# The third pair's weights loaded as six whole chunks in place of 22 halves and pieces

## The chip, the cores and the metric

One NeuronCore of a Trainium2 chip runs the kernel. The metric is the time on the device in microseconds; lower is better.

## What is computed

One inference step of a decoder layer, for a prompt of 256 positions and 8 sample rows, width 1024, all in float32. First come a combined input projection, a short gated convolution, a windowed attention and an output projection. Then comes a mixture of experts: each row chooses 4 of 32 experts, and each expert is an up-projection of 1024 x 2048, a clamped SwiGLU and a down-projection of 1024 x 1024:

```
u = xb @ w_up[e] + b_up[e]
glu = jnp.minimum(u[:, 0::2], SWIGLU_LIMIT)
lin = jnp.clip(u[:, 1::2], -SWIGLU_LIMIT, SWIGLU_LIMIT)
a = glu * jax.nn.sigmoid(SWIGLU_ALPHA * glu) * (lin + 1)
return a @ w_down[e] + b_down[e]
```

The results of an expert are weighted by its gate and added to the rows that chose it. The change is in the loading of the experts' weights, 32 x 12 MiB = 403 MB.

## The kernel before

The experts are worked through in 16 pairs, g = 0 to 15. A pair's weights are six chunks of 4 MiB: four of the up-projections (two for each expert) and two of the down-projections. A chunk is 128 partitions x 32 KB, and it is used in two halves, j = 0 to 11 in a pair: half j is chunk j // 2, its first or second 16 KB of every partition. On TensorE `up(j)` reads j = 0 to 7 (L2009) and `down(e, h)` reads j = 8 to 11 (L2076). Both ask `loaded(j)` (L1975) to wait for the half; between them stand the gathering of the next pair's rows, the transposes and the scattering of results, in an order written out by hand (L2182 to L2238).

**Four places.** In SBUF there are places for four chunks (`unit(u)`, L347): three in the tile `ring`, one in `area`. Chunk number `turn`, counted from the second pair on, takes the place `UNIT[turn % 4]`, so it can be loaded when the chunk four ahead of it has been read. All loads are issued by SP on one queue, in the order of use, and each waits on SP for a semaphore that counts releases by TensorE, `ring_free`. A release is signalled by the matmul that comes after the last read of a half or, from the third pair on, of a chunk (`frees(j)`, L1996).

**How the loads are cut.** SP has a section for each kind of pair:

- The first pair (g = 0, L605 to L638) is loaded in halves, two of them in smaller parts.
- The second pair (g = 1, L639 to L649) is loaded in halves (16 KB of each partition), but its j = 10 and 11 in two pieces each.
- The third pair (g = 2, L650 to L664) is loaded in pieces and halves. Its chunks 0 to 3 take the places that the second pair's chunks 2 to 5 leave. Its chunks 4 and 5 take the places of its own chunks 0 and 1. `EARLY` (L209) tells in how many pieces: 4 for the second half of chunk 0, which follows j = 5, and 2 for each other half. `early` (L585) issues each piece but the last when the matmuls that read that much of the place are through (`early_free`); the last one waits for `ring_free`. The halves of chunks 4 and 5 wait for `chunk_free` and `ring_free`.
- The pairs g = 3 to 14 run in a loop (`pair`, L598): each chunk is one DMA, whole, after one wait.
- The last pair is loaded in halves and in rows (`LAST_ROWS`, L212), so that the last matmuls can follow the last bytes.

The second pair in `pair()` on TensorE has `halves=True, pair1=True` (L2293), the third `halves=True, pair2=True` (L2294); both wait for each half and, where there are pieces, for `early_piece` (L1984).

Of the kernel before, what the change touches and what calls it, by code (L numbers as in the profile page):

```python
# [56 lines left out]
PAIR_CHUNKS = UP_CHUNKS + DOWN_CHUNKS  # L57
# [9 lines left out]
UNIT = [1, 2, 3, 0]  # L67
UNITS_KEPT = len(UNIT)
ODD, EVEN = 0, -PAIR_CHUNKS
assert 2 * PAIR_CHUNKS % UNITS_KEPT == 0  # L70
PAIRS2_TURNS = 2 * PAIR_CHUNKS // UNITS_KEPT
HALF_PAIRS = (1, 2)
PAIR1_FREED = HALF_FREED + len(FIRST_PLACE)
LOOP_FREED = PAIR1_FREED + 2 * PAIR_CHUNKS - PAIR_CHUNKS

# [130 lines left out]
OUTPUTS = [(0, 0), (1, 0), (0, 1), (1, 1)]  # L206


EARLY = {2: 2, 3: 2, 4: 2, 5: 4, 6: 2, 7: 2, 8: 2, 9: 2, 10: 2, 11: 2}  # L209


LAST_ROWS = {7: (2, 2), 8: (2, 2), 9: (2, 2), 10: (2, 2), 11: (2, 1, 1)}  # L212
# [23 lines left out]
def build(nc, x_prompt, x_sample, state_conv, cache_k, cache_v, rel_bias, attn_norm_w, w_in, conv_w, q_norm_w,  # L236
          k_norm_w, sinks, w_out, ffn_norm_w, w_router, b_router, w_up, b_up, w_down, b_down, consts,
          y_prompt, y_sample, conv_prompt, k_prompt, v_prompt, conv_sample, k_sample, v_sample):
    with ExitStack() as ctx:
# [3 lines left out]
        def sem(name):  # L243
            return ctx.enter_context(nc.semaphore(name))
# [165 lines left out]
        ring_free = sem("ring_free")  # L410
        first_loaded = [sem(f"first_loaded{j}") for j in range(2 * PAIR_CHUNKS)]
        unit_half = [sem(f"unit_half{u}") for u in range(UNITS_KEPT)]
# [84 lines left out]
        last_piece = {(j, n): sem(f"last_piece{j}_{n}") for j, rows_ in LAST_ROWS.items() for n in range(len(rows_) - 1)}  # L497
        y_first = sem("y_first")
        early_free = sem("early_free")
        chunk_free = sem("chunk_free")  # L500
        first_free = sem("first_free")
        early_piece = {j: sem(f"early_piece{j}") for j in EARLY}
        sample_cleared = sem("sample_cleared")
# [36 lines left out]
        def _(sp):  # L540
# [12 lines left out]
            for c in range(2, FIRST_CHUNKS):  # L553
# [4 lines left out]
                else:  # L558
                    n = c - W_IN_CHUNKS
# [19 lines left out]
            def half(b, i, turn, h):  # L579

                u = UNIT[turn % UNITS_KEPT]
                f = slice(SLOT * h, SLOT * h + SLOT)
                sp.dma_start(unit(u)[:, f], rows_of(b, i)[:, f]).then_inc((unit_half, unit_full)[h][u], 16)

            def early(b, i, turn, h, j, freed):  # L585

                u = UNIT[turn % UNITS_KEPT]
                size = SLOT // EARLY[j]
                for n in range(EARLY[j]):
                    f = slice(SLOT * h + size * n, SLOT * h + size * n + size)  # L590
                    if n == EARLY[j] - 1:
                        sp.wait_ge(ring_free, freed)
                        sp.dma_start(unit(u)[:, f], rows_of(b, i)[:, f]).then_inc((unit_half, unit_full)[h][u], 16)
                    else:
                        sp.wait_ge(early_free, sum(EARLY.get(c, 1) - 1 for c in range(j)) + n + 1)
                        sp.dma_start(unit(u)[:, f], rows_of(b, i)[:, f]).then_inc(early_piece[j], 16)
# [42 lines left out]
            for b in range(PAIR_CHUNKS):  # L639
                for h in range(2):  # L640
                    if b < UNITS_KEPT:
                        sp.wait_ge(ring_free, FREED[2 + 2 * b + h])
                    else:
                        j = 2 * (b - UNITS_KEPT) + h
# [5 lines left out]
            for b in range(PAIR_CHUNKS):  # L650
                turn = PAIR_CHUNKS + b
                freed = turn - UNITS_KEPT
                for h in range(2):
                    j = 2 * freed + h
                    if j in EARLY:
                        early(b, 2, turn, h, j, PAIR1_FREED + j + 1)
                        continue
                    if freed < PAIR_CHUNKS:
                        sp.wait_ge(ring_free, PAIR1_FREED + j + 1)
                    elif h == 0:  # L660
                        sp.wait_ge(chunk_free, freed - PAIR_CHUNKS + 1)
                    else:
                        sp.wait_ge(ring_free, LOOP_FREED + freed + 1)
                    half(b, 2, turn, h)  # L664
            with sp.Fori(1, PAIRS // 2 - 1) as h:
                pair(h, 1, h * 2 + 1)
                pair(h + 1, 0, h * 2 + 2)
            for b in range(PAIR_CHUNKS):
                turn = 2 * PAIR_CHUNKS * (PAIRS // 2 - 1) + ODD + b
                sp.wait_ge(ring_free, LOOP_FREED + turn - UNITS_KEPT + 1)  # L670
                u = UNIT[turn % UNITS_KEPT]
                for h in range(2):
                    j = 2 * b + h
# [905 lines left out]
        def _(pe):  # L1579
# [32 lines left out]
            for what, a in STEPS:  # L1612
                if what == "anorm":
                    tr(misc_bank()[:, 0:KT], rows[V_ANORM:V_ANORM + KT, :]).then_inc(misc_full, 1)
                elif what == "s_cols":
                    b = misc_bank()
                    pe.wait_ge(x_sample_loaded, 16)
                    for k in range(KT):
                        mm = tr(b[:, DEC * k:DEC * k + DEC], x[0:DEC, 2, 128 * k:128 * k + 128])
                    mm.then_inc(misc_full, 1)  # L1620
                    for m, h in TURNS:
                        pe.wait_ge(x_loaded[m][h], 16)
                        for k in range(4 * h, 4 * h + 4):
                            o = 1024 * m + 128 * k
                            mm = tr(pA[:, o:o + 128], x[:, m, 128 * k:128 * k + 128])
                        mm.then_inc(x_halves, 1)
                elif what == "rstd":
                    b = misc_bank()
                    pe.wait_ge(norm_inv, 1)
                    for m, (t0, r) in enumerate(TOK):  # L1630
                        mm = matmul(b[:, t0:t0 + r], stat[0:r, 12 + m:13 + m].to_broadcast([r, 128]), ident[0:r, 0:r])
# [7 lines left out]
                elif what == "tile":  # L1639
                    kind, c, j, t = TILES[a]  # L1640
# [9 lines left out]
                    for k in range(KT):  # L1650
                        if c == 0:
# [5 lines left out]
                            mm = matmul(pB[:, a % 2, 0:NT], w, xw[:, k, :], start=(k == 0), stop=(k == KT - 1))  # L1657
# [7 lines left out]
                        if kind != "q":  # L1665
                            w = ring[:, place(c), :].rearrange("p (k n) -> p k n", k=KT)[:, k, 128 * j:128 * j + 128]
                            mm = matmul(pB[:, a % 2, 0:NT], w, hT[:, k, :], start=(k == 0), stop=(k == KT - 1))
# [4 lines left out]
                        for h in range(2):  # L1672
                            mm = matmul(pB[HD * h:HD * h + HD, a % 2, 0:NT], w[:, k, h, HD * j:HD * j + HD],
                                        hT[:, k, :], start=(k == 0), stop=(k == KT - 1))
# [287 lines left out]

            pe.wait_ge(bias_cast, SPLITS)

            def pair(g, pairs2, odd, kind, halves=False, pair1=False, pair2=False, left_over=None):
                first, last = kind == "first", kind == "last"
                base = {"first": PRE_FILLS, "over": OVER_BASE + PAIR_FILLS * g}.get(kind, PAIR_BASE + PAIR_FILLS * g)
                parity = {"first": PRE_FILLS, "over": OVER_BASE}.get(kind, PAIR_BASE) % 2
# [6 lines left out]
                def loaded(j, whole=False):  # L1975

                    b, h = j // 2, j % 2
                    if first:
                        pe.wait_ge(first_loaded[j], {8: 64, 9: 32}.get(j, 16))
                        return first_place(j)  # L1980
                    turn = (ODD if odd else EVEN) + b
                    u = UNIT[turn % UNITS_KEPT]
                    early_j = PAIR_CHUNKS * 2 * (g - 1) + j - 2 * UNITS_KEPT if halves else -1
                    if early_j in EARLY:  # L1984
                        pe.wait_ge(early_piece[early_j], 16 * (EARLY[early_j] - 1))
                    if last and j in LAST_ROWS and not whole:
                        pe.wait_ge(last_piece[j, 0], 16)
                    elif (last or halves) and h == 0:
                        n = 1 + len(HALF_PAIRS) * PAIR_CHUNKS // UNITS_KEPT if last else 1
                        at_ = turn if last else PAIR_CHUNKS * (g - 1) + b  # L1990
                        pe.wait_ge(unit_half[u], 16 * (n + at_ // UNITS_KEPT))
                    elif last or halves or h == 0:
                        pe.wait_ge(unit_full[u], 16 * PAIRS2_TURNS * pairs2 + 16 * (turn // UNITS_KEPT + 1))
                    return unit(u)[:, SLOT * h:SLOT * h + SLOT]
# [14 lines left out]
                def up(j, freed=False):  # L2009

                    e = j // UP_CHUNKS
                    c = j % UP_CHUNKS
                    if first and e == 0:
                        if c == 1:
                            first_turn(2)
                            first_turn(3)
                        pe.wait_ge(misc_free, FILL["x_turn", c])
                    elif j in (0, 2):
                        pe.wait_ge(misc_free, base - 1 + j // 2 - (1 if pair1 else 0))
                    w = loaded(j)  # L2020
                    for k in (2 * c, 2 * c + 1):
                        if last and j in LAST_ROWS and k % 2:
                            loaded(j, whole=True)
                        row = w[:, 2048 * (k % 2):2048 * (k % 2) + 2048]
                        for n in range(2):
                            for a in range(2):
                                mm = matmul(up_out(e, a, n), xsT[:, k, 64 * e:64 * e + 64], columns_of(row, a, n),
                                            start=(k == 0), stop=(k == KT - 1))
                                if freed and k == 2 * c and n == a == 0:
                                    mm.then_inc(ring_free, 1)  # L2030
                                if first and j == 0 and a and n == 0:
                                    mm.then_inc(first_free, 1)
                                if pair1 and a and EARLY.get(j) == 4 and (k % 2, n) != (1, 1):
                                    mm.then_inc(early_free, 1)
                        if pair1 and EARLY.get(j) == 2 and k % 2 == 0:
                            mm.then_inc(early_free, 1)
                        if first and j == k == 0:
                            mm.then_inc(ring_free, 1)
                        elif first and j == 1 and k == 2:
                            mm.then_inc(first_free, 1)  # L2040
                    if c == UP_CHUNKS - 1:
                        mm.then_inc(up_done, 1)
                    elif frees(j):
                        mm.then_inc(ring_free, 1)
                    elif pair2 and j in (0, 2):
                        mm.then_inc(chunk_free, 1)

                def y_rows(e, a):

# [241 lines left out]

            left_over = pair(0, 0, 0, "first")
            pair(1, 0, 1, "steady", halves=True, pair1=True, left_over=left_over)  # L2293
            pair(2, 1, 0, "steady", halves=True, pair2=True)  # L2294
            with pe.Fori(1, PAIRS // 2 - 1) as h:
                pair(h * 2 + 1, h, 1, "steady")
                pair(h * 2 + 2, h + 1, 0, "steady")
# [44 lines left out]
```

## Time and profile before

| | |
|---|---|
| time, median of 3 runs | 1174.58 us (1174.53 to 1174.8) |
| profiled execution: its span | 1172.1 us (no other time of it is given) |
| TensorE busy | 1121.6 us, 96% |
| VectorE, ScalarE, GpSimd busy | 35%, 16%, 1% |
| DMA | 442.03 MB, mean 377 GB/s |
| mean granted TensorE clock | 0.994 of full speed |

The span goes from the first to the last instruction. The profile's page has busy shares over the whole span and in 40 equal slices; TensorE's share there is modelled, so 96% is not 96% of what the engine can do. The other views are answers of the trace: windows (busy time, DMA share and GB/s in any stretch), the waits of an engine and what ended them, the chain of waits (the work that ended last, followed back), the list of instructions in time, and the DMA issues with the time until their data had landed. A DMA is spread over 16 DMA engines and has landed when the last of them is through.

### The profile page before, as it was taken

What the parts mean: (1) busy time and instruction counts of PE and PEld (TensorE: products, weight loads), DVE (VectorE), ACT (ScalarE), POOL (GpSimd) and SP (SyncE); (2) the same over time, 40 slices, a digit from 0 to 9 for tenths busy, and PEclk for the clock granted to TensorE, in tenths of its full rate; (3) what the DMA queues carried; (4) which work ended last, traced back from release to release, by engine and by line L of the source; (5) the groups of instructions that cost most, each with busy time, mean ns of one, the idle gap of its engine ahead of it and who ended that gap; (6) DMA issues with size and microseconds to landing.
All of it is one profiled execution on the core that took longest, in us unless ns stands there. A gap on an engine that the chain in (4) does not pass through costs nothing.

```text
span 1172.1 us, 14019 instructions
## 1 busy us (share of the span) xinstructions
PE 1121.6 (96%) x5671; PEld 502.1 (43%) x5671; DVE 414.4 (35%) x848; ACT 191.4 (16%) x363; POOL 16.5 (1%) x31
## 2 busy tenths in 40 slices
PE   9999999999999999999999999999999999999998
PEld 6688888663333333333333333333333333333332
DVE  4763354663263323323131323232323232322222
ACT  2123213431042010101011111111010101010101
POOL 1200001000000000000000000000000000000000
PEclk9999999999999999999999999999999999999999
DMA  9945325839999999999999999999999999999997
GB/s 318 372 168 179 130 88 201 342 127 397 428 420 423 431 428 431 430 430 432 431 431 435 433 433 431 431 432 429 435 434 432 431 432 431 431 433 434 426 422 289
DMA packets 41870, 442.03 MB, mean 377 GB/s; under 512 B 3890, under 2 KB 9266, under 8 KB 24828
## 3 DMA queue, kind: packets, MB, share of 16 engines
q1 hardware_dynamic: 39336, 435.08, 88.7%
q0 software_dynamic: 1648, 5.83, 1.6%
q10 hardware_dynamic: 852, 0.64, 0.2%
q8 instruction: 26, 0.43, 0.1%
q14 instruction: 8, 0.07, 0.0%
HBM read 440.23 MB, written 2.36 MB: 378 GB/s over the span
## 4 chain that ended last, share of the span: by engine, by line
PE 60%; DMA 36%; DVE 2%; ACT 1%; issue 0%; SPq 0%; ACTq 0%
PE pA L1589 26%; PE pB L1589 26%; DMA ring<-in_w_up 18%; DMA ring<-in_w_down 12%; PE pM L1589 6%; DMA area<-in_w_up 5%; PE pM L1592 1%; PE pA L1592 1%; DMA rows<-in_attn_norm_w 0%; ACT area L942 0%; DVE hn L1483 0%; DVE x L1441 0%; DVE area L1485 0%; DVE area L1477 0%; DVE area L1020 0%
## 5 line engine op out<-in xcount | busy, mean ns | idle before, releaser
L1589 PE MATMUL pA<-ring,hn 128*64 128x512 f32 x1536 | 352.6, 602 | 23.4 <-DMA ring<-in_w_up 23.4
L1589 PEld LDWEIGHTS pA<-ring,hn 128*64 128x64 f32 x1536 | 105.2, 137 | 219.3 <-issue 185.5
L1589 PE MATMUL pB<-area,ring 128*128 128x264 f32 (+1 forms) x928 | 184.6, 388 | 0.3 <-ACT area L794 0.3
L1589 PE MATMUL pB<-ring,area 128*64 128x512 f32 (+2 forms) x784 | 171.5, 591 | 7.1 <-DMA ring<-in_w_down 5.8
L1589 PEld LDWEIGHTS pB<-area,ring 128*128 128x128 f32 (+1 forms) x928 | 143.6, 175 | 34.4 <-issue 3.0
L1589 PE MATMUL pA<-area,hn 128*64 128x512 f32 x512 | 119.3, 610 | 10.4 <-DMA area<-in_w_up 10.4
L1589 PEld LDWEIGHTS pB<-ring,area 128*64 128x64 f32 (+2 forms) x784 | 58.6, 136 | 101.9 <-issue 89.0
L1441 DVE TENSOR_TENSOR x<-pM,x 128x512 f32<-128x512 f32 x60 | 40.1, 691 | 147.3 <-PE pM L1589 147.2
L930 ACT ACTIVATE area<-area 128x512 f32<-128x512 f32 x30 | 18.9, 630 | 385.2 <-DVE area L1424 385.2
L1356 DVE COPY conv_row<-pM 128x512 f32<-128x512 f32 x30 | 20.6, 686 | 146.4 <-PE pM L1589 146.4
L1589 PE MATMUL pB<-area 128*64 128x512 f32 (+2 forms) x300 | 66.9, 549 | 1.2 <-DVE area L1007 1.2
L1589 PEld LDWEIGHTS pA<-area,hn 128*64 128x64 f32 x512 | 36.1, 139 | 74.6 <-issue 59.7
L1589 PE MATMUL pM<-area 128*128 128x512 bf16 (+2 forms) x368 | 52.4, 330 | 1.5 <-DVE x L1441 1.4
L1424 DVE TENSOR_SCALAR area<-pA 128x512 f32<-128x512 f32 x30 | 20.7, 691 | 92.6 <-PE pA L1589 92.6
L1359 DVE TENSOR_TENSOR hn<-pM,fnorm 128x512 f32<-128x512 f32 x30 | 20.7, 691 | 84.9 <-PE pM L1592 84.4
L1466 DVE COPY area<-pB 64x512 f32<-64x512 f32 x15 | 10.4, 694 | 101.5 <-PE pB L1589 101.5
L1589 PEld LDWEIGHTS pM<-area 128*128 128x128 bf16 (+2 forms) x368 | 18.7, 96 | 52.4 <-issue 35.6
L1589 PE MATMUL pM<-hn,x 128*128 128x512 bf16 (+1 forms) x120 | 37.4, 396 | 0.0
L1589 PEld LDWEIGHTS pB<-area 128*64 128x64 f32 (+2 forms) x300 | 20.8, 131 | 35.3 <-issue 30.7
L1592 PEld LDWEIGHTS pA<-cst,area 128*128 128x128 f32 x168 | 22.2, 190 | 24.8 <-issue 24.3
L942 ACT ACTIVATE area<-pA 128x512 f32<-128x512 f32 x15 | 9.0, 597 | 120.7 <-PE pA L1592 120.7
L1592 PE MATMUL pA<-cst,area 128*128 128x128 f32 x168 | 28.3, 299 | 0.0
(307 smaller groups left out, 788.0 us busy)
## 6 DMA issues: line engine op xcount, KB each, us to landing
ring<-in_w_up SPq DMA_DIRECT2D x36, 4096.0 KB, 29.8
ring<-in_w_down SPq DMA_DIRECT2D x18, 4096.0 KB, 29.1
area<-in_w_up SPq DMA_DIRECT2D x12, 4096.0 KB, 30.2
ring<-in_w_up SPq DMA_DIRECT2D x17, 2048.0 KB, 13.3
area<-in_w_down SPq DMA_DIRECT2D x6, 4096.0 KB, 30.0
ring<-in_w_in SPq DMA_DIRECT2D x22, 1024.0 KB, 12.7
ring<-in_w_up SPq DMA_DIRECT2D x14, 1024.0 KB, 9.3
ring<-in_w_down SPq DMA_DIRECT2D x13, 1024.0 KB, 25.9
```

The costliest lines, as they stand in the source:

```text
L930: nc.scalar.activation(early_sig if kind == "first" else sig[:, e, :], early_glu if kind == "first" else glu[:, e, :], ACT.Sigmoid, scale= ...
L942: nc.scalar.activation(turned, pA[:, 1024:1536], ACT.Copy).then_inc(aT_ready, 1)
L1356: return V.tensor_copy(xrow[:, 512 * half:512 * half + 512], b)
L1359: return V.tensor_tensor(xsT[:, 4 * half:4 * half + 4, :], b.rearrange("p (k s) -> p k s", k=4), fw[:, 4 * half:4 * half + 4, :], ALU.mult)
L1424: V.tensor_scalar(gl, u[:, 0, e], LIMIT, None, ALU.min).then_inc(glu_ready, 1)
L1441: V.tensor_tensor(xo, bank(k), xo, ALU.add).then_inc(misc_free, 1)
L1466: V.tensor_copy(y_pair[64:128, 512:1024], pB[64:128, 1, :]).then_inc(y_ready_dve, 1)
L1589: return pe.matmul(out, w, m, start=start, stop=stop, skip_group_check=True)
L1592: return pe.transpose(out, src, ident[0:src.shape[0], 0:src.shape[0]])
```

## The change

SP loads each of the third pair's six chunks with one DMA (`whole`, L574), after one wait on `ring_free` for the last half of the chunk that held the place. `EARLY` keeps only j = 2 and 3, which concern the second pair. TensorE runs the third pair like the pairs of the loop: it waits once for a chunk, on `unit_full`, and signals a release once for a chunk. `chunk_free` goes, and the number of halves that the last pair counts on is worked out anew (`HALVES_OF`).

```diff
--- before.py
+++ after.py
@@ -69,7 +69,7 @@
 ODD, EVEN = 0, -PAIR_CHUNKS
 assert 2 * PAIR_CHUNKS % UNITS_KEPT == 0
 PAIRS2_TURNS = 2 * PAIR_CHUNKS // UNITS_KEPT
-HALF_PAIRS = (1, 2)
+HALVES_OF = [sum(UNIT[b % UNITS_KEPT] == u for b in range(PAIR_CHUNKS)) for u in range(UNITS_KEPT)]
 PAIR1_FREED = HALF_FREED + len(FIRST_PLACE)
 LOOP_FREED = PAIR1_FREED + 2 * PAIR_CHUNKS - PAIR_CHUNKS
 
@@ -206,7 +206,7 @@
 OUTPUTS = [(0, 0), (1, 0), (0, 1), (1, 1)]
 
 
-EARLY = {2: 2, 3: 2, 4: 2, 5: 4, 6: 2, 7: 2, 8: 2, 9: 2, 10: 2, 11: 2}
+EARLY = {2: 2, 3: 2}
 
 
 LAST_ROWS = {7: (2, 2), 8: (2, 2), 9: (2, 2), 10: (2, 2), 11: (2, 1, 1)}
@@ -497,7 +497,6 @@
         last_piece = {(j, n): sem(f"last_piece{j}_{n}") for j, rows_ in LAST_ROWS.items() for n in range(len(rows_) - 1)}
         y_first = sem("y_first")
         early_free = sem("early_free")
-        chunk_free = sem("chunk_free")
         first_free = sem("first_free")
         early_piece = {j: sem(f"early_piece{j}") for j in EARLY}
         sample_cleared = sem("sample_cleared")
@@ -650,18 +649,11 @@
             for b in range(PAIR_CHUNKS):
                 turn = PAIR_CHUNKS + b
                 freed = turn - UNITS_KEPT
-                for h in range(2):
-                    j = 2 * freed + h
-                    if j in EARLY:
-                        early(b, 2, turn, h, j, PAIR1_FREED + j + 1)
-                        continue
-                    if freed < PAIR_CHUNKS:
-                        sp.wait_ge(ring_free, PAIR1_FREED + j + 1)
-                    elif h == 0:
-                        sp.wait_ge(chunk_free, freed - PAIR_CHUNKS + 1)
-                    else:
-                        sp.wait_ge(ring_free, LOOP_FREED + freed + 1)
-                    half(b, 2, turn, h)
+                if freed < PAIR_CHUNKS:
+                    sp.wait_ge(ring_free, PAIR1_FREED + 2 * freed + 2)
+                else:
+                    sp.wait_ge(ring_free, LOOP_FREED + freed + 1)
+                whole(b, 2, turn)
             with sp.Fori(1, PAIRS // 2 - 1) as h:
                 pair(h, 1, h * 2 + 1)
                 pair(h + 1, 0, h * 2 + 2)
@@ -1962,7 +1954,7 @@
 
             pe.wait_ge(bias_cast, SPLITS)
 
-            def pair(g, pairs2, odd, kind, halves=False, pair1=False, pair2=False, left_over=None):
+            def pair(g, pairs2, odd, kind, halves=False, pair1=False, left_over=None):
                 first, last = kind == "first", kind == "last"
                 base = {"first": PRE_FILLS, "over": OVER_BASE + PAIR_FILLS * g}.get(kind, PAIR_BASE + PAIR_FILLS * g)
                 parity = {"first": PRE_FILLS, "over": OVER_BASE}.get(kind, PAIR_BASE) % 2
@@ -1986,9 +1978,8 @@
                     if last and j in LAST_ROWS and not whole:
                         pe.wait_ge(last_piece[j, 0], 16)
                     elif (last or halves) and h == 0:
-                        n = 1 + len(HALF_PAIRS) * PAIR_CHUNKS // UNITS_KEPT if last else 1
-                        at_ = turn if last else PAIR_CHUNKS * (g - 1) + b
-                        pe.wait_ge(unit_half[u], 16 * (n + at_ // UNITS_KEPT))
+                        n = HALVES_OF[u] if last else 0
+                        pe.wait_ge(unit_half[u], 16 * (n + b // UNITS_KEPT + 1))
                     elif last or halves or h == 0:
                         pe.wait_ge(unit_full[u], 16 * PAIRS2_TURNS * pairs2 + 16 * (turn // UNITS_KEPT + 1))
                     return unit(u)[:, SLOT * h:SLOT * h + SLOT]
@@ -2042,8 +2033,6 @@
                         mm.then_inc(up_done, 1)
                     elif frees(j):
                         mm.then_inc(ring_free, 1)
-                    elif pair2 and j in (0, 2):
-                        mm.then_inc(chunk_free, 1)
 
                 def y_rows(e, a):
 
@@ -2291,7 +2280,7 @@
 
             left_over = pair(0, 0, 0, "first")
             pair(1, 0, 1, "steady", halves=True, pair1=True, left_over=left_over)
-            pair(2, 1, 0, "steady", halves=True, pair2=True)
+            pair(2, 1, 0, "steady")
             with pe.Fori(1, PAIRS // 2 - 1) as h:
                 pair(h * 2 + 1, h, 1, "steady")
                 pair(h * 2 + 2, h + 1, 0, "steady")
```

## Rows read from the trace of the kernel before

**Rows 1.** The page: busy shares of the engines, and the 40 slices.

```profile
PE 1121.6 (96%) x5671; PEld 502.1 (43%) x5671; DVE 414.4 (35%) x848; ACT 191.4 (16%) x363; POOL 16.5 (1%) x31
...
DMA  9945325839999999999999999999999999999997
GB/s 318 372 168 179 130 88 201 342 127 397 428 420 423 431 428 431 430 430 432 431 431 435 433 433 431 431 432 429 435 434 432 431 432 431 431 433 434 426 422 289
```

**Rows 2.** Windows: us, busy by engine, PEclk, DMA share, GB/s.

```profile
...
256.00:258.40 2.40, 2.40 (x16) 2.11 (x14) 1.62 (x8) 0.00 (x0) 0.00 (x0) 1.00 0.00 0
258.40:341.20 82.80, 80.07 (x399) 31.76 (x400) 31.43 (x95) 17.23 (x28) 0.00 (x0) 1.00 0.98 408
343.10:402.60 59.50, 59.30 (x293) 21.08 (x290) 21.09 (x37) 11.20 (x17) 0.00 (x0) 1.00 1.02 425
402.60:440.00 37.40, 37.20 (x177) 13.34 (x177) 11.80 (x20) 5.48 (x9) 0.00 (x0) 1.00 1.00 428
440.00:1155.00 715.00, 675.37 (x3275) 241.79 (x3271) 207.04 (x355) 83.13 (x137) 0.00 (x0) 0.99 1.00 431
```

**Rows 3.** TensorE's waits in 426:540, then 540:780, then 780:1110 us.

```profile
PE pB L1589 <- ACT area L942: 0.4, 2, 0.2
...
PE pA L1589 <- DMA ring<-in_w_up: 7.3, 6, 1.9
PE pA L1589 <- DMA area<-in_w_up: 3.7, 2, 1.9
PE pB L1589 <- DMA ring<-in_w_down: 1.9, 4, 0.5
...
PE pA L1589 <- DMA ring<-in_w_up: 16.1, 16, 1.9
PE pA L1589 <- DMA area<-in_w_up: 6.6, 5, 1.9
PE pB L1589 <- DMA ring<-in_w_down: 2.9, 6, 0.5
```

**Rows 4.** The chain of waits: start us, us, what; the pairs' first matmuls.

```profile
372.35 4.02 PE pA L1589 x20
...
425.71 4.02 PE pA L1589 x20
...
479.07 4.02 PE pA L1589 x20
...
558.38 30.30 DMA area<-in_w_up
```

**Rows 5.** The chain of waits in the last 45 us.

```profile
1129.26 25.86 DMA ring<-in_w_down
...
1155.24 1.94 PE pB L1589 x8
```

**Rows 6.** Single DMA issues, KB, us to landing: at 258.40, 333.35, 390.23 us.

```profile
ring<-in_w_up SPq DMA_DIRECT2D x1, 2048.0 KB, 7.2
...
ring<-in_w_down SPq DMA_DIRECT2D x1, 1024.0 KB, 9.8
...
ring<-in_w_down SPq DMA_DIRECT2D x1, 2048.0 KB, 12.4
```

**Rows 7.** SP's issues in 326:400 us: start us, us, line, transfer.

```profile
333.35 0.33 SPq L593 DMA_DIRECT2D ring<-in_w_down  x1
...
334.22 0.33 SPq L596 DMA_DIRECT2D area<-in_w_up  x1
...
345.04 0.33 SPq L593 DMA_DIRECT2D area<-in_w_up  x1
...
354.56 0.33 SPq L593 DMA_DIRECT2D ring<-in_w_up  x1
...
372.01 0.33 SPq L593 DMA_DIRECT2D ring<-in_w_up  x1
...
398.32 0.36 SPq L577 DMA_DIRECT2D ring<-in_w_up  x1
```

## Prediction

> **What bounds the kernel now.** I read first the page's busy shares and its 40 slices [rows 1]. TensorE is busy 96% of the span, which would make it the bound; but the slices show the DMA engines full from the tenth slice to the last but one, at about 430 GB/s. So two things are full and the stages have to be told apart. The windows [rows 2] do that: the queue is empty from 256 to 258.4 us, and after that no stretch up to 1155 us has a DMA share under 0.98. The waits of TensorE on loads [rows 3] give the other half: in 426 to 540 us it waits for no load at all (its longest sum is 0.4 us, on another engine); in 540 to 780 us it waits 12.9 us for loads (7.3 + 3.7 + 1.9), in 780 to 1110 us 25.6 us. The chain [rows 4] has the pairs starting at 372.35, 425.71 and 479.07 us, 53.36 us apart, and at 558.38 us it enters a DMA that it had not touched for 200 us.
>
> Read together: a pair costs TensorE 53.36 us. It loads 24 MiB, 25.17 MB, which at the 431 GB/s of 440 to 1155 us [rows 2] takes 58.4 us. At 372 us TensorE has loads in hand; it eats 5 us of this lead a pair and has none by about 560 us. From then on the loads set the pace up to the end, where TensorE still waits for the row pieces of the last chunk [rows 5]: it starts at 1155.24 us on a DMA of 25.86 us, and works on without a stop to speak of. **So whatever time the DMA queue loses or gains after 260 us comes out at the end**, TensorE's lead at the moment of the loss notwithstanding.
>
> **The change, part by part.** It touches the six chunks of the third pair (g = 2). Before, the first four of them go out as 14 pieces of 1 MB and four of 0.5 MB, each when its own piece of the place has been read, and the last two as four halves: 22 DMAs. After, there are 6.
>
> *Bytes in larger rows: a gain.* The piece before the third pair's first (issued 333.35 us, 9.8 us to landing [rows 6]) lands at 343.15 us. The third pair's last half (390.23 us, 12.4 us [rows 6]) lands at 402.6 us. Between them lie exactly its 25.17 MB: 59.5 us, and the window of that stretch says the same, 425 GB/s [rows 2]. As whole rows, at 431 GB/s, they take 58.4 us. Gain: 1.1 us.
>
> *The first whole chunk goes out later: a loss.* The first chunk was issued from 334.22 us in pieces, the last of them at 345.04 us [rows 7]. That last piece waited for the same count of releases (`ring_free` for j = 5) as the whole chunk now waits for, and TensorE's work up to there depends on nothing that is changed. So the whole chunk is issued at 345.04 us. What bridges the time until then? Only what was issued up to 333.35 us. From the empty queue at 258.40 us that is 32 MiB, 33.55 MB (2 + 2 MB, six pieces that make 4 MB, eight halves of the second pair, two more halves and four 1 MB pieces). At 408 GB/s over 82.8 us, 33.8 MB have been moved by 341.2 us [rows 2], these and a little other traffic: the average engine has run out there, and the last of the 16 by 343.15 us, when the piece is reported landed. Before, the pieces issued from 334.22 us on follow directly.
>
> Starting an empty queue costs time too. The half at 258.40 us met one and took 7.2 us [rows 6]; its 2.10 MB are 4.9 us at 431 GB/s, so 2.3 us are start and finish. The new chunk's bytes thus run as if from 347.4 us. Idle: 4.2 us for the last engine (347.4 - 343.15), 6.2 us for the average one (347.4 - 341.2). The lower end is where the start costs no more than the issue itself, 0.33 us [rows 7]: 2.2 us.
>
> *Is there a second hole?* The chunk lands 9.7 us after 347.4, at 357.1 us. The next is issued at 354.56 us, 2.5 us ahead, against a start of 2.3: just covered. The fourth goes out at 372.01 us and the next pair's first at 398.32 us [rows 7], while the chunks before them land at 376.5 and 405.7 us: covered with more each time, by the queued bytes.
>
> *TensorE's waits.* It now waits for a whole chunk where it waited for a half or a piece. It starts the third pair at 372.35 us [rows 4] and the first chunk is there at 357.1; each later chunk lands 9.7 us after the one before and is wanted some 8.9 us (53.36 / 6) after it, so the sixth has still 11 us. Cost: nothing, while this lead lasts. The signals and waits dropped on TensorE cost nothing either: the pair with them takes the same 53.36 us as the two loop pairs after it [rows 4]. On SP nothing but the same loads stands behind the longer waits.
>
> *The sum.* By the last engine 4.2 - 1.1 = +3.1 us; by the average engine 6.2 - 1.1 = +5.1; by the shortest start 2.2 - 1.1 = +1.1. TensorE is released when the last engine has landed, in both kernels, so I take a value near that end, +3.4: the 0.3 is for the engines restarting level, so that those that were early have lost more and later stray traffic can make one of them the last. The page gives no time of its own beside the span of 1172.1 us; the median of the runs, 1174.58, is 2.5 us above it, and I let that stand. **1174.58 + 3.4 = 1178.0 us.**
>
> **A rule weighed against the rows.** The rows say that 16 more DMAs cost 1.1 us in all, because pieces queue behind each other: 0.07 us each. The Trainium skill, DMA: Bandwidth & Descriptors, Anatomy of one DMA, gives each DMA a fixed 2.0 us beside its bytes (fitted there for the GpSimd path), and Rules for kernel authors says to coalesce transfers; taken as a sum of costs, 16 DMAs fewer would bring 32 us and the kernel to about 1142. The 22 pieces run at 425 GB/s, so the traces are against it.
>
> **The rivals.** A measurement of this kernel tells about 0.2%, 2.35 us, from no change.
>
> *The lead covers the hole (not slower).* TensorE has some 14 us of loads in hand when the hole comes. If the loads made the 4.2 us up later, only the gain would be left: 1174.58 - 1.1 = 1173.5 us, or 1174.6 if that is lost as well. It decides if the queue had idle time before that a late load could use. Rows 2 speak against it: 428 GB/s right after, 431 from there to the end, share 1.00. 0.1.
>
> *The hole is as wide as the average engine sees it.* Each engine is set back by its own idle time, and the last at the end is one of those that were early at 341 us: +5.1, 1179.7 us. For it: such an engine loses 6.2. Against it: the engines of before do not land together either, and the last one counts. 0.2.
>
> *The start is short.* If an engine begins right after the issue, +1.1 gives 1175.7 us, which is within the 0.2%. Against it stands the 7.2 us of [rows 6]. 0.05.
>
> *Each DMA has a cost that doesn't overlap.* In [rows 6] a start costs 2.3 us; if every piece paid it, 16 of them would give back 37 us and the kernel would take 1141 us. The 425 GB/s with 22 DMAs is against it. 0.02.
>
> **How the numbers follow.** The forecast has 0.63. The range runs from the shortest start, 1175.7, to the average engine, 1179.7. Slower by over 0.2% (above 1176.9): the forecast, the wide hole and a little of the rest, 0.84. Within 0.2%: the lead's cover and the short start, 0.14. Faster: 0.02.
>
> **What would show it.** The whole chunk issued near 345.0 us, 12.1 us to landing; DMA share near zero at some point between 343 and 346 us; 343 to 403 us no longer at 425 but at some 431 GB/s once the queue runs again; the pairs still 53.36 us apart at first, and TensorE's first wait for a load some 35 us sooner (3.4 of 5 us a pair); the tail's DMA landing at about 1158.6 in place of 1155.1 us. I am wrong if the queue is not empty at 345 us, if the whole chunk goes out earlier, or if the last landing does not move by the hole less the gain.

## The result and the profile after

The changed kernel took 1180.09 us, the median of 4 runs (1178.96 to 1180.91), against 1174.69 for the kernel before: +5.4 us, a ratio of 1.0046 (95% interval 1.0033 to 1.0058). I had forecast slower, 1178.0 us, with a range up to 1179.7. The direction held; the size was too small by 2.0 us, and the time lies 0.4 us outside the range. The profiled execution was the fastest of the four, 1178.96 us with a span of 1177.2. Of all the executions, one of first_pieces ran slow (1287.49 us, at a granted clock of 0.85 where the others had 0.99 or more), and it is left out.

The page first: the span, the engines, and the slices that stand in [rows 1].

```profile
span 1177.2 us, 13968 instructions
...
PE 1116.5 (95%) x5642; PEld 502.7 (43%) x5671; DVE 414.6 (35%) x848; ACT 191.5 (16%) x363; POOL 16.6 (1%) x31
...
DMA  9945425839989999999999999999999999999997
GB/s 320 372 163 177 138 86 202 332 143 400 429 348 413 433 431 429 429 434 432 432 430 434 431 432 431 434 431 432 429 436 429 433 430 435 430 432 431 426 424 288
```

The span is 5.1 us longer. TensorE's busy time is 5.1 us shorter, but the trace also has 29 matmul records fewer, so that difference says nothing of its work. The 12th slice (324 to 353 us) moved 348 GB/s where it had moved 420. Windows (us, busy by engine, PEclk, DMA share, GB/s) narrow it down; the first line is of the kernel before, the others are of the changed one.

```profile
...
341.20:345.00 3.80, 3.80 (x22) 1.38 (x20) 3.70 (x8) 1.15 (x2) 0.00 (x0) 1.00 1.01 418
...
341.20:345.00 3.80, 3.80 (x22) 1.37 (x20) 3.70 (x8) 1.15 (x2) 0.00 (x0) 1.00 0.03 13
343.10:402.60 59.50, 58.92 (x290) 21.08 (x290) 21.09 (x37) 11.20 (x17) 0.00 (x0) 1.00 0.95 402
356.00:358.50 2.50, 2.50 (x14) 1.02 (x15) 2.37 (x6) 0.00 (x0) 0.00 (x0) 1.00 0.89 328
406.00:440.00 34.00, 33.64 (x161) 12.15 (x160) 11.11 (x19) 5.48 (x9) 0.00 (x0) 1.00 1.00 431
440.00:1155.00 715.00, 667.42 (x3234) 241.44 (x3255) 207.10 (x355) 82.37 (x135) 0.00 (x0) 0.99 1.00 431
```

From 341.2 to 345.0 us the queue is all but empty: a share of 0.03 in place of 1.01. The stretch that ran at 425 GB/s before [rows 2] now runs at 402. A second, shallow dip lies at 356 to 358.5 us: 328 GB/s. From 406 us on everything is as before, 431 GB/s to the end; nothing is made up. SP's list of issues (start, us, line, transfer) answers to [rows 7].

```profile
333.33 0.33 SPq L592 DMA_DIRECT2D ring<-in_w_down  x1
...
345.04 0.33 SPq L576 DMA_DIRECT2D area<-in_w_up  x1
...
354.56 17.79 SPq L576 DMA_DIRECT2D ring<-in_w_up  x3
...
380.06 0.33 SPq L576 DMA_DIRECT2D area<-in_w_down  x1
...
398.32 10.08 SPq L576 DMA_DIRECT2D ring<-in_w_up  x2
```

The 18 pieces between 334.22 and 372.01 us are gone, and so are the four halves behind them. The first chunk is issued at 345.04 us, the very moment at which its last piece was. The single issues at 333.33, 345.04 and 354.56 us (KB, us to landing), as in [rows 6]:

```profile
ring<-in_w_down SPq DMA_DIRECT2D x1, 1024.0 KB, 9.5
...
area<-in_w_up SPq DMA_DIRECT2D x1, 4096.0 KB, 12.2
...
ring<-in_w_up SPq DMA_DIRECT2D x1, 4096.0 KB, 13.9
```

The last piece ahead of the hole lands at 342.8 us, the first chunk at 357.2, the second at 368.5. The chain of waits (start, us, what) answers to [rows 4] and [rows 5].

```profile
372.35 4.02 PE pA L1581 x20
...
425.71 4.02 PE pA L1581 x20
...
478.87 26.80 DMA ring<-in_w_up
...
1133.67 26.15 DMA ring<-in_w_down
...
1159.96 1.94 PE pB L1581 x8
```

The third and the fourth pair start at 372.35 and 425.71 us, to the hundredth as before. TensorE did not notice the hole; its lead did. The chain now goes through a load issued at 478.87 us, where before the first such load was issued at 558.38. In the tail the piece that TensorE waits for lands at 1159.82 us (1133.67 + 26.15) in place of 1155.12.

### The profile page after: what moved, and what is told of

Same layout as the page of the kernel before. It is cut to its first block, busy times and chain, and to the rows that moved or that the text cites. A ratio compares the mean times of both kernels' runs of the same rounds, so it can differ in the third digit from the quotient of the medians.

```text
span 1177.2 us, 13968 instructions
## 1 busy us (share of the span) xinstructions
PE 1116.5 (95%) x5642; PEld 502.7 (43%) x5671; DVE 414.6 (35%) x848; ACT 191.5 (16%) x363; POOL 16.6 (1%) x31
## 4 chain that ended last, share of the span: by engine, by line
PE 55%; DMA 41%; DVE 2%; ACT 1%; issue 1%; ACTq 0%; SPq 0%
PE pB L1581 25%; PE pA L1581 23%; DMA ring<-in_w_up 20%; DMA ring<-in_w_down 12%; DMA area<-in_w_up 8%; PE pM L1581 5%; PE pM L1584 1%; PE pA L1584 1%; DMA x<-in_x_prompt 1%; ACT area L934 0%; DVE x L1433 0%; DVE hn L1475 0%; DVE area L1477 0%; DVE area L1469 0%; DVE area L1012 0%
## 5 line engine op out<-in xcount | busy, mean ns | idle before, releaser
L1581 PE MATMUL pM<-area 128*32 128x256 bf16 (+2 forms) x353 | 49.0, 327 | 3.9 <-issue 2.4
L1581 PE MATMUL pM<-hn,x 128*128 128x512 bf16 (+1 forms) x106 | 34.2, 396 | 2.1 <-issue 2.1
```

The costliest lines, as they stand in the source:

```text
L1581: return pe.matmul(out, w, m, start=start, stop=stop, skip_group_check=True)
```

## Experiments

Two theories stood against each other at first. **Queue:** time for which the DMA queue is idle after 260 us comes out at the end in full. **Lead:** the loads that TensorE has in hand cover it, and the cost lies elsewhere, as in TensorE's waits for whole chunks. Later the question was which idle time counts: that of the average engine, of the last one, and whether the stalls behind the first hole belong to it.

### The same kernels again: after_again, before_again

No edit.

> The changed kernel once more, for a second profile and a tighter interval. Queue theory (idle time of the DMA queue after 260 us comes out at the end in full): +5.4 us over the kernel before, 1.0046, with the first hole at 341 to 347 us again and a shorter stall of the engines near 356.5 us. If the last landing of the profile taken first (+4.7 us) is typical and the other runs were chance, +4.3 us.

1179.49 us (1179.19 to 1179.99, 5 runs) against 1174.37: +5.1 us, ratio 1.0041 (1.0028 to 1.0055). So +5.4 was no chance, and 5.1 to 5.4 is the size to explain.

> The kernel before once more, for a second profile: how far the last of the 16 DMA engines is behind at 343 us and at the end, if nothing is changed. The time as before, 1174.0 to 1175.7; the last piece lands some 11.5 us ahead of the measured end, as in every kernel run so far.

1174.0 us, a single run. Its trace gives the second line of the table in the section on the prediction.

### A larger hole: one_later, three_later

```diff
-                    sp.wait_ge(ring_free, PAIR1_FREED + 2 * freed + 2)
+                    sp.wait_ge(ring_free, PAIR1_FREED + 2 * freed + 2 + (b == 0))
```

(three_later: `+ 3 * (b == 0)`.)

> The changed kernel, but the third pair's first chunk waits for one release more: issued at 348.47 in place of 345.04 us. Queue theory: the first hole grows by 3.4 us and the stall at 356.5 us goes (the second chunk's issue is now 5.9 us ahead of the first one's landing), so 2.8 to 3.4 us more than the changed kernel, some +8.5 over before. Rival, the lead of TensorE covers what comes late: no more than the changed kernel. Rival, the cost lies in TensorE's waits for whole chunks: as the changed kernel, since the same waits are there.

1182.21 us (1181.77 to 1182.29, 5 runs), ratio 1.0065 (1.0051 to 1.0078): 2.7 us over the changed kernel measured beside it, just under the 2.8 to 3.4 expected, and +7.8 over before. The windows show the hole, and no dip at the landing of the first chunk, which the average engine now has at 360.4 us:

```profile
...
341.20:345.00 3.80, 3.80 (x24) 1.34 (x20) 3.70 (x8) 1.15 (x2) 0.00 (x0) 1.00 0.04 17
345.00:347.20 2.20, 2.20 (x14) 0.76 (x12) 1.50 (x4) 0.63 (x1) 0.00 (x0) 1.00 0.00 0
347.20:349.00 1.80, 1.80 (x12) 0.70 (x9) 0.02 (x1) 1.69 (x2) 0.00 (x0) 1.00 0.00 0
351.00:357.00 6.00, 6.00 (x30) 2.22 (x28) 3.25 (x6) 2.17 (x3) 0.00 (x0) 1.00 1.01 437
359.50:362.00 2.50, 2.50 (x14) 0.86 (x12) 0.00 (x0) 0.00 (x0) 0.00 (x0) 1.00 0.98 413
440.00:1155.00 715.00, 668.74 (x3245) 240.43 (x3241) 205.19 (x349) 82.32 (x135) 0.00 (x0) 0.99 1.00 431
```

From 345 to 349 us not a byte moves; at 351 to 357 and at 359.5 to 362 the queue is full. The hole grew by 3.5 us and the time by 2.7; the vanished dip would account for the difference. The waits for whole chunks are the same as in the changed kernel, so they are not what the 2.7 us are. Nor do they cost there: in the changed kernel TensorE waits for no load between 372 and 480 us.

> The changed kernel, but the third pair's first chunk waits for three releases more: issued at 359.82 in place of 345.04 us. Queue theory: 14.8 us more hole, the later stalls gone, so 14 us more than the changed kernel, some +19.5 over before (1194), though TensorE's lead of some 14 us is about as long as that. Rival, the lead covers a hole as far as it reaches: a few us at most over before, since the first chunk would land at 371.9 us and is wanted at 372.35.

1192.57 us (1191.8 to 1193.39, 4 runs) against 1174.64: +17.9 us, ratio 1.0153 (1.0138 to 1.0169).

```profile
...
341.20:345.00 3.80, 3.80 (x24) 1.34 (x20) 3.70 (x8) 1.15 (x2) 0.00 (x0) 1.00 0.07 26
351.00:357.00 6.00, 6.00 (x30) 2.22 (x28) 3.24 (x7) 2.17 (x3) 0.00 (x0) 1.00 0.00 0
440.00:1155.00 715.00, 664.98 (x3225) 239.48 (x3223) 205.20 (x348) 81.13 (x133) 0.00 (x0) 0.99 1.00 431
```

The whole lead is spent at once: TensorE waits for loads already in the third pair, 372 to 430 us, where it waited for none before.

```profile
PE pA L1581 <- DMA ring<-in_w_up: 2.9, 2, 1.6
```

These are 2.9 us there, and 0.6 us more on `ring<-in_w_down`; from 430 to 540 us it waits another 9.7 us for loads, again where it waited for none before. The theory of the lead falls. The expected 19.5 us came out 1.6 short; the table in the section on the prediction says where.

### The hole moved: first_pieces

The first chunk goes out in pieces as before (`EARLY` keeps 4: 2 and 5: 4), the other five whole.

```diff
-EARLY = {2: 2, 3: 2}
+EARLY = {2: 2, 3: 2, 4: 2, 5: 4}
+CUT = [0]
```

(`CUT` names the chunks that are not loaded whole; the code that reads it is shown with the next experiment.)

> The third pair's first chunk in pieces as before, the other five whole. Queue theory: the hole moves. The first chunk's last piece lands at 351.5 us for the average engine, the second chunk is issued at 354.56 and its bytes run from 356.9: 5.4 us idle and a stall of some 0.4 behind it, less 0.9 us gained by long rows: +4.9 over before, 1179.6, about as the changed kernel. Rival, only the chunk that comes first out of a nearly empty queue matters: 0.9 us faster than before, 1173.8.

1178.86 us (1178.47 to 1179.16, 4 runs) against 1174.64: +4.2 us, ratio 1.0035 (1.0021 to 1.005). The expected 4.9 came 0.7 short; the rival, 0.9 us faster than before, falls.

```profile
...
341.20:345.00 3.80, 3.80 (x22) 1.37 (x20) 3.70 (x7) 1.15 (x2) 0.00 (x0) 1.00 1.03 420
351.00:357.00 6.00, 6.00 (x30) 2.21 (x29) 3.24 (x6) 2.17 (x3) 0.00 (x0) 1.00 0.37 111
356.00:358.50 2.50, 2.50 (x14) 0.97 (x14) 2.47 (x6) 0.00 (x0) 0.00 (x0) 1.00 0.70 275
```

No hole at 341 to 345 us any more, but one at 351 to 357: share 0.37. The first chunk is nothing special: here it is the second one, now the first to wait for a whole place, that lets the queue run dry.

### Halves, and only the last two whole: four_halves, four_pieces

Chunks 0 to 3 as halves (`half` behind the release of each), chunks 4 and 5 whole; and chunks 0 to 3 in pieces as before, 4 and 5 whole.

```diff
+CUT = [0, 1, 2, 3]
...
+                if b in CUT:
+                    for h in range(2):
+                        j = 2 * freed + h
+                        if j in EARLY:
+                            early(b, 2, turn, h, j, PAIR1_FREED + j + 1)
+                            continue
+                        sp.wait_ge(ring_free, PAIR1_FREED + j + 1)
+                        half(b, 2, turn, h)
+                    continue
```

(Left out: on TensorE the waits for these halves, one by one. four_pieces has the same lines, with the `EARLY` of the kernel before.)

> Chunks 0 to 3 of the third pair in halves of 16 KB rows, each after the release of its own half; chunks 4 and 5 whole. Queue theory: the half for j = 4 goes out at 335.94 us and lands for the average engine at 346.1; the one for j = 5 at 345.04 us starts the bytes at 347.3: 1.2 us of hole, some 0.5 us of stalls behind it, 1.0 us gained by longer rows: +0.7 us over before, 1175.4. If the late whole chunks cost by TensorE's waits and not by the queue, the same 1175 would come, but with the hole absent from the trace.

1175.96 us (1175.39 to 1177.46, 11 runs) against 1174.37: +1.6 us, ratio 1.0012 (1.0003 to 1.0021). The hole is there, small:

```profile
...
345.00:347.20 2.20, 2.20 (x12) 0.70 (x10) 1.50 (x4) 0.63 (x1) 0.00 (x0) 1.00 0.88 283
```

By the medians it cost 0.9 us more than I had said; the interval, 0.4 to 2.5 us, takes in the 0.7 as well.

> Chunks 0 to 3 of the third pair in pieces as before, only chunks 4 and 5 whole. Queue theory: chunk 4 is issued at 380.06 us, when the last piece before it lands at 381.3 for the average engine (383.0 for the last); its bytes run from 382.4: 1.1 us of hole, some 0.5 of stall ahead of chunk 5 (390.23 against a landing at 392.4), 0.1 gained: +1.5 over before, 1176.2. Rival, the last engine's landing counts: the hole is nothing, +0.0 to +0.4.

1175.09 us (1173.75 to 1176.65, 11 runs) against 1174.64: +0.45 us, ratio 1.0002 (0.9993 to 1.0011). 1.5 us were expected of the queue theory, 0 to 0.4 of its rival, by which the last engine's landing counts. The interval, -0.8 to +1.3 us, leaves out the 1.5 and takes in the rival's: a miss for the queue theory as I had priced it. The traced execution (1175.31 us) has the dip (0.83 at 378 to 381 us, then 388 GB/s), and in it the third pair's last chunk lands 1.6 us later for the average engine than in the kernel before; the eleven runs spread over 2.9 us, and why their median is only 0.45 us later stays open.

```profile
...
378.00:381.00 3.00, 3.00 (x15) 0.93 (x12) 0.15 (x1) 0.00 (x0) 0.00 (x0) 1.00 0.83 344
381.00:384.00 3.00, 3.00 (x15) 0.92 (x14) 1.18 (x2) 0.00 (x0) 0.00 (x0) 1.00 1.05 388
384.00:400.00 16.00, 16.00 (x88) 5.54 (x86) 5.57 (x10) 1.23 (x2) 0.00 (x0) 1.00 1.00 411
```

### The stalls behind the hole: second_halves, halves_12

The changed kernel with its second chunk, or its second and third, in halves; edit as above with `CUT = [1]` and `CUT = [1, 2]`, and the short `EARLY`.

> The changed kernel, but the second of the third pair's chunks in two halves: the first half is issued at 348.47 us and is in the queue when the first chunk lands. Theory that the surplus over my 3.4 us is in part the stall of the engines at 356.5 us (second chunk issued 2.4 us ahead of the landing): the stall goes, 0.5 to 0.7 us less than the changed kernel, +4.8 over before. Rival, the surplus is all in the first hole: as the changed kernel.

1179.50 us (1178.49 to 1179.69, 5 runs): no less than the changed kernel's 1179.49. A miss. The traced execution is the fastest of the five, and in it the stalls are gone: from the first chunk's landing to the third pair's last the average engine needs 48.6 us, five chunks at full rate.

> The changed kernel, but its second and third chunks in halves, so that the queue has something at every landing behind the first hole. Theory that the stalls behind the first hole (some 1.1 us for the average engine in the changed kernel's trace) cost time: 0.5 to 1.0 us less than the changed kernel, 1178.6 to 1179.0. Rival, the first hole is all of it: as the changed kernel, 1179.5.

1178.89 us (1178.83 to 1179.11, 5 runs) against 1174.40: +4.5 us, ratio 1.0035 (1.0021 to 1.0048). That is 0.6 us less than after_again and within what I expected, and its runs lie all below those of after_again; but the intervals overlap, and second_halves showed nothing. That the stalls cost some tenths is possible, not shown. The windows are the hole as in the changed kernel, and a shallower dip behind it (360 GB/s in place of 328).

```profile
...
341.20:345.00 3.80, 3.80 (x24) 1.34 (x20) 3.70 (x8) 1.15 (x2) 0.00 (x0) 1.00 0.03 13
356.00:358.50 2.50, 2.50 (x15) 0.99 (x15) 2.46 (x6) 0.00 (x0) 0.00 (x0) 1.00 0.84 360
```

### The rows alone: loop_quarters

The kernel before, with each loop chunk as four DMAs of 8 KB rows behind one wait.

```diff
+                    for n in range(4):
+                        f = slice(SLOT // 2 * n, SLOT // 2 * n + SLOT // 2)
+                        sp.dma_start(unit(u)[:, f], rows_of(b, i)[:, f]).then_inc(unit_full[u] if n == 3 else unit_part[u], 16)
```

> The kernel before, but each chunk of the pairs in the loop (12 pairs) is issued as four DMAs of 8 KB rows at the same moment, behind the same wait: 216 DMAs more, the rows of the pieces, no hole. Row theory: the stretch of pieces ran at 425 GB/s against 431, 1.1 us a pair, so +13 us; up to +20 if 8 KB rows alone are slower than the mixed stretch. Rival, each DMA has a fixed 2 us beside its bytes: +430 us. Rival, the length of the rows does nothing and the stretch was slow for other reasons: no change.

1190.70 us (1190.43 to 1190.98, 4 runs) against 1174.64: +16.1 us, ratio 1.0136 (1.0121 to 1.0152). The first line is of the kernel before.

```profile
...
440.00:1073.00 633.00, 596.37 (x2887) 213.89 (x2883) 182.28 (x309) 73.78 (x121) 0.00 (x0) 0.99 1.00 432
...
343.10:402.60 59.50, 59.30 (x292) 20.97 (x289) 21.33 (x37) 11.21 (x17) 0.00 (x0) 1.00 1.01 421
440.00:1073.00 633.00, 580.23 (x2812) 215.49 (x2813) 179.86 (x306) 73.77 (x121) 0.00 (x0) 0.99 1.01 422
```

The loop runs at 422 GB/s in place of 432, with the queue always full. 16.1 us over 12 pairs are 1.3 us a pair: the price of cutting a pair into 8 KB rows, and about what the change gains once. The run changes the rows and the number of DMAs together; the packets speak for the rows, with 313 ns for 8 KB against 1215 for 32 KB, 3% more a byte. Over 216 more DMAs it is 0.07 us each. The Trainium skill, DMA: Bandwidth & Descriptors, Anatomy of one DMA, gives each DMA a fixed 2.0 us, fitted there for the GpSimd path. No such cost shows here, on SP's queue with other loads always queued.

## Why the prediction was wrong in its size

Each of the 16 DMA engines signals when its share of a transfer has landed. From these signals in the traces, the landing of the average (median) engine and of the last one, in us (`changed` is the first profile of the changed kernel):

```
                piece before the hole   first chunk       third pair's last   the last piece
before          341.41 / 343.14         -                 400.99 / 402.59     1160.54 / 1162.56
before_again    341.26 / 342.54         -                 400.93 / 401.96     1161.25 / 1162.68
changed         341.16 / 342.84         356.92 / 357.19   406.62 / 408.32     1166.04 / 1167.27
after_again     340.99 / 343.05         356.85 / 357.27   406.90 / 408.54     1166.18 / 1168.43
halves_12       341.21 / 342.99         357.06 / 357.26   405.79 / 407.49     1165.39 / 1167.52
second_halves   341.20 / 343.09         357.02 / 357.21   405.66 / 407.35     1165.22 / 1167.15
one_later       341.29 / 343.00         360.42 / 362.23   409.02 / 410.64     1168.64 / 1170.68
three_later     340.97 / 343.47         371.80 / 372.18   420.40 / 422.14     1180.08 / 1180.55
four_pieces     341.04 / 343.02         -                 402.60 / 404.06     1162.16 / 1163.58
```

In the eleven profiled executions whose time is known, the end comes 11.3 to 11.7 us after the last column's second number, in every variant. The time goes with the landing of the last engine, as I had said.

**Right: the bound and the chain of cause.** The queue is full from 260 us on and a hole in it is not filled later: one_later and three_later add 3.5 and 14.9 us of hole (the average engine lands the first chunk at 360.4 and 371.8 us, against 356.9) and 2.7 and 12.8 us of time. That the change would be slower, and why, was no luck.

**Right: the times of the step.** Issue at 345.04 us as forecast; landing after 12.2 us where I had 12.1; the third and fourth pair unmoved; nothing on TensorE.

**Right: the gain of the long rows.** I had 1.1 us by the windows. By the landings it is 1.3: the third pair takes the average engine 59.6 us before (341.41 to 400.99), and six whole chunks at the changed kernel's 9.71 us (396.91 to 406.62, the last two landings of the pair) take 58.3.

**Wrong: the hole by the last engine.** The step was: TensorE is released when the last engine has landed, in both kernels, so the hole is the last engine's 4.2 us and not the average engine's 6.2, with 0.3 us for stray traffic. The release is as I had it; the conclusion is not. In the kernel before, the last engine is 1.3 to 1.7 us behind the average at 343 us. The hole makes them start nearly level: 0.2 to 0.4 us at the first chunk's landing in five of the six rows that have one. The last engine's own hole is then 4.6 us (357.19 - 342.84 less 9.7 us for a chunk; 4.5 in after_again), close to my 4.2, and had the engines stayed level, my sum would about have held.

But 50 us later the last one is 1.6 to 1.7 us behind again, and 1.2 to 2.3 us at the end (0.5 in three_later), as in the kernel before (1.4 and 2.0). A restart does not wipe this distance out for good; so the shift at the end is close to that of the average engine. Its hole, 356.92 - 341.16 less the 9.7 us of a chunk at 431 GB/s, is 6.0 us, and 6.2 - 1.1 = +5.1 is the rival to which I had given 0.2. It does not hold everywhere: four_pieces came out nearer to the last engine's price, and in three_later the distance came back least (0.5 us at the end). There the average engine's last landing is 18.8 to 19.5 us later than in the two profiles of before, about the 19.5 us that I expected, and the time only 17.9.

What brings the distance back stands in the packets of the traces. Some 25 us apart, packets of 16 KB of the queue that fetches instructions pass through one engine each, as here one between 357.3 and 362.5 us in halves_12:

```profile
...
q8 instruction: 1, 0.02, 1.2%
```

It takes 1.0 us (from 360.57 us), and the weights' packet that starts as it ends takes 1078 ns in place of 611. That sets one engine back by 1.5 us. In second_halves all 16 engines land within 0.22 us of the average at 357.02 us; the fetch starts at 360.36, and at the next landing, 361.90 us, one engine is 1.55 us behind while the other fifteen stay within 0.21. In one_later the fetch (360.20 us) comes while the first chunk is still under way, and its last engine is 1.8 us behind at that landing already. three_later is the counterpart: this fetch falls into the hole, at 357.80 us, where no weights move, and the last engine is 0.4 and 0.6 us behind at the landings of 371.80 and 381.55 us. It is 1.6 us behind only at the landing after the next fetch, which starts at 388.54 us. The stray traffic to which I had given 0.3 us is thus what a restart cannot escape. A trace does not name a packet's engine, so this is read from the times alone, and no run was made to move the fetches. They also spread the times: at 1146 us one fetch takes the last engine's distance in after_again from 1.4 to 2.4 us, in the changed kernel's first profile only from 1.1 to 1.2, which would account for the 1.0 us between those two executions.

**Wrong, smaller: no second hole.** I had the second chunk covered, 2.5 us of margin against a start of 2.3. The windows show the dip at 356 us, and between the first chunk and the third pair's last the average engine needs 49.7 us in the changed kernel, 48.7 in halves_12. That is 1.0 us of stalls, a term that I had put at nothing, as just covered. What they are worth in the time is not settled: halves_12 is 0.6 us faster than after_again, second_halves not at all.

**Too small: when the lead runs out.** I had TensorE's first wait for a load some 35 us sooner. In the kernel before it stands at 559.6 us (540:560, the first line), in the changed one at 505.7 us (500:520, the second): 54 us sooner.

```profile
PE pA L1589 <- DMA ring<-in_w_up: 0.7, 1, 0.7
...
PE pA L1581 <- DMA ring<-in_w_up: 0.2, 1, 0.2
```

A hole of 6.0 us with stalls of 1.0, less 1.3 us of gain, is 5.7 us, and at 5 us a pair that is some 60 us. The measure is coarse: before_again has a first wait of 0.2 us at 540.4 us already.

By the terms, then: 6.0 + 1.0 - 1.3 = +5.7 us for the average engine at the end of the third pair (406.62 - 400.99 gives 5.6); +5.1 to +5.4 in the time, which goes by whichever engine is last.

## What to carry to other kernels

Find the point after which a transfer queue never runs dry. If the loads set the pace at the end, a hole behind that point comes out there nearly in full, even where its consumer has work enough in hand not to notice it (one_later: no wait for a load before 488 us, and yet 7.8 us of time for a hole of 9.4 us less 1.3 of gain). Waiting for a larger place to become free is then worth it only while the bytes already queued outlast the wait and the start of a new transfer: here short rows cost 1.3 us for 24 MiB, and the hole that they avoided cost 6. When a hole is priced, start from the average engine's idle time and not from the last one's: that the engines start level behind the hole is soon undone.

## What the runs showed of the hardware

- A chunk that is issued 2.4 us ahead of the landing of the one before it still leaves a dip (328 GB/s for 2.5 us in the changed kernel); in one_later, where the margin was 5.8 us, there is next to none (413 GB/s at 359.5 to 362 us, share 0.98).
- Loads in rows of 8 KB in a full queue run at 422 GB/s, in rows of 32 KB at 432 (loop_quarters against the kernel before).
- Behind a hole the engines start nearly level (the last one lands 0.2 to 0.4 us behind the average at the next landing), and one fetch of 16 KB by the instruction queue sets one engine back by 1.5 us: 1.0 us of its own, and 0.47 us by which the next packet on that engine is longer. A fetch that falls into the hole sets none back (three_later).
